# Low parts of the u table in the gate stage: every second block on GpSimd instead of VectorE

## What is computed

```python
a = jax.nn.gelu(jnp.einsum('td,tkd->tk', xt, u_tab[it]))   # it: 8 heads x 16 experts of 16384, per token
y = jnp.einsum('tk,tkd->td', gt * a, v_tab[it])
```

## Time and profile before

| what | value |
|---|---|
| median of 3 runs | 2208.14 us (2207.04 to 2209.24) |
| the profiled execution: its time, its span | 2208.77 us, 2207.0 us |
| busy over the span | PE 93%, DVE 69%, ACT 37%, POOL 31% |
| the chain that ended last | PE 72%, DMA 9%, DVE 8%, issue 5%, ACT 4%, POOL 1% |
| gate stage | from 943 to 1426 us of the span |

### The profile page before, as it was taken

The page is one execution under the profiler, slowest core; times in us unless marked ns, Lnnn a source line. Parts: engine busy times, 40 slices in busy tenths (PEclk is TensorE's granted clock), DMA queues, the critical chain, the costliest instruction groups (busy, mean ns, idle before and its releaser), DMA issues.

```text
span 2207.0 us, 28461 instructions
## 1 busy us (share of the span) xinstructions
PE 2043.3 (93%) x9877; PEld 1635.1 (74%) x9877; DVE 1524.7 (69%) x3164; ACT 822.6 (37%) x1507; POOL 693.4 (31%) x469
## 2 busy tenths in 40 slices
PE   6999999697998989988888889979999999999998
PEld 2554454544998989887787788878888888888886
DVE  4222315624689999988788877738877678778776
ACT  2111004223222323377777778723222232222222
POOL 0000001002223666543333322214434355545451
PEclk8999999798999999999999999989999999999999
DMA  9121204415111455579999988989999899999994
GB/s 336 61 77 38 82 0 152 153 72 200 39 39 53 157 180 159 157 274 350 344 358 358 347 308 316 333 334 340 398 338 346 289 348 328 347 334 343 335 344 164
DMA packets 183919, 526.01 MB, mean 238 GB/s; under 512 B 16775, under 2 KB 67111, under 8 KB 181256
## 3 DMA queue, kind: packets, MB, share of 16 engines
q1 hardware_dynamic: 128520, 323.41, 40.5%
q0 software_dynamic: 55296, 201.35, 25.5%
HBM read 460.48 MB, written 64.23 MB: 238 GB/s over the span
## 4 chain that ended last, share of the span: by engine, by line
PE 72%; DMA 9%; DVE 8%; issue 5%; ACT 4%; POOL 1%; SPq 0%; ACTq 0%; DVEq 0%; POOLq 0%
PE ps L1012 32%; PE ps L945 12%; DMA ugat<-in_u_rows,idxs 6%; PE ps L662 5%; DVE junk L1477 3%; PE ps L755 3%; PE ps L881 3%; PE ps L917 3%; PE ps L918 3%; PE ps L721 3%; PE ps L985 2%; DMA uraw<-in_u_t 2%; DVE eA L1495 2%; ACT uhi L1737 2%; DMA wring<-in_w_ada 2%
## 5 line engine op out<-in xcount | busy, mean ns | idle before, releaser
L945 PE MATMUL ps<-h2hi,uhi 128*128 128x384 f32 x1024 | 400.9, 392 | 39.3 <-issue 19.7
L1885 POOL DMA_INDIRECT ugat<-in_u_rows,idxs x256 | 272.6, 1065 | 520.4 <-DVE dots L1477 509.5
L1012 PE MATMUL ps<-vhi,whi 128*128 128x512 f32 x1024 | 399.2, 390 | 5.1 <-DVE wlo L1524 5.1
L1012 PE MATMUL ps<-vhi,wlo 128*128 128x512 f32 x1024 | 398.8, 389 | 0.0
L1012 PE MATMUL ps<-vlo,whi 128*128 128x512 f32 x1024 | 398.8, 389 | 0.0
L945 PE MATMUL ps<-h2lo,uhi 128*128 128x384 f32 x1024 | 351.9, 344 | 0.0
L945 PE MATMUL ps<-h2hi,ulo 128*128 128x384 f32 x1024 | 349.8, 342 | 0.0
L1815 ACT ACTIVATE vhi<-vraw 128x1024 fp32r<-128x1024 f32 x128 | 135.5, 1061 | 463.6 <-PE ps L1012 442.8
L1893 POOL DMA_INDIRECT vgat<-in_v_tab,idxs x128 | 217.1, 1696 | 220.5 <-DVE y L1535 177.6
L985 PE MATMUL ps<-eA,eB 128*128 128x128 f32 x1024 | 213.5, 291 | 55.0 <-DVE eA L1495 46.6
L985 PEld LDWEIGHTS ps<-eA,eB 128*128 128x128 f32 x1024 | 182.7, 194 | 93.9 <-DVE eA L1495 66.2
(11 more groups left out here) (275 smaller groups left out, 3063.2 us busy)
## 6 DMA issues: line engine op xcount, KB each, us to landing
uraw<-in_u_t SPq DMA_DIRECT2D x128, 512.0 KB
vraw<-in_v_tab SPq DMA_DIRECT2D x128, 512.0 KB
gate_scratch<-gst SPq DMA_DIRECT2D x16, 2048.0 KB
gin<-gate_scratch SPq DMA_DIRECT2D x32, 1024.0 KB
wring<-in_w_ada SPq DMA_DIRECT2D x12, 2048.0 KB, 10.3
gelu_scratch<-aout SPq DMA_DIRECT2D x128, 192.0 KB
ain<-gelu_scratch SPq DMA_DIRECT2D x32, 768.0 KB, 7.4
wring<-in_w_in SPq DMA_DIRECT2D x6, 2048.0 KB, 8.4
```

What stands on the lines that cost most here:

```text
L945: last = pe.matmul(ps[:, b % 4, 0:TA], w[:, b % 2, k, :], h[:, k, LP:LP + TA], start=(k == 0 and j == 0), stop=(k == KD - 1 and j == 2))
L1012: last = pe.matmul(ps[:, y_bank(t) + h, :], w[:, b, (t - 1) * P:t * P], v[:, b, h * 512:(h + 1) * 512], start=(start and j == 0), stop=(st ...
L1885: pool.indirect_dma_start(out=ugat[:, g % GSLOT], out_offset=None, in_=u_rows, in_offset=bass.IndirectOffsetOnAxis(ap=idxs[:, g // HK, g % ...
```

## The change

GpSimd makes the low part of every even block from 54 to 116 (32 of the 64 that VectorE made). Its program takes up the part of block n + 1 ahead of the gathers that follow the dots of block n. VectorE leaves these out, and ahead of each low part that it still makes it waits until GpSimd's last one is done; GpSimd waits likewise for VectorE's. One such wait stands before block 116's successor too. GpSimd's `split_u` is the function that it has for blocks 0 to 52; it waits for `uhi` of the block and for `h_full`.

```diff
+def pool_low(n):
+    return BLK_A < n <= BLK_C and n % 2 == 0
...
-                    if k == 3:
+                    if k == 3 and not pool_low(n + 1):
+                        dve.wait_ge(ulo_ready, n + 1)
                         split_u(n + 1, n + 1)
...
+            dve.wait_ge(ulo_ready, BLK_C + 1)
             for n in range(BLK_C, NBLK):
...
             pool.wait_ge(idx_ready, 2)
-            for g in range(GSLOT, NDOT):
+            for n in range(BLK_A, BLK_C):
+                if pool_low(n + 1):
+                    pool.wait_ge(ulo_ready, n + 1)
+                    split_u(n + 1, n + 1, False)
+                for g in dots_at(n):
+                    gather_u(g + GSLOT)
+            for g in range(dots_before(BLK_C) + GSLOT, NDOT):
                 gather_u(g)
```

## The result

The changed kernel takes 2243.55 us (median of 4, 2241.53 to 2246.82), the one before beside it 2207.59 us (2199.4 to 2209.24): a ratio of 1.0172 with an interval of 1.0149 to 1.0194. That is 36 us slower; forecast were 8.5 us, and at most 26. The profiled execution has a span of 2245.0 us, 38 us longer than before.

The account below looks back on a forecast made before the run. Bound: a 6.92 us loop over the low part in two-dot blocks, full VectorE in three-dot blocks, transfers near. +10.7 - 6.5 + 4.3 = +8.5 us on 2208.77 gave 2217.3 us; own range 2213 to 2225, 8-in-10 range 2200 to 2234.

Parts of the forecast that it names:

- What VectorE loses per subtraction: Gate stage: each GpSimd subtraction makes VectorE stand still for 2.07 us, tiles and dots alike.
- The gathers' constant 937 ns: Gather instructions took 936 to 937 ns in nearly all of 166 cases, though starting beside tiles; evidence against stopped tiles.
- Three-dot blocks: Gate blocks with three dots, 19 pairs: VectorE is full, odd blocks go from 6.92 to 7.6 us; +10.7 us.
- the cover by transfers: Three-dot pairs: a quarter cost nothing because transfers set the pace; +10.7 us with it, 14 without.
- Two-dot blocks: Gate blocks with two dots, 13 pairs: VectorE no longer idles for the high part, block about 6.4 us; -6.5 us.
- Lock and loop: Gate stage: subtractions stopping VectorE in three-dot pairs, +10.7 us, and the shortened wait chain in two-dot pairs, -6.5 us.
- the queue of GpSimd: Three-dot pairs: gathers queue behind the high-part wait and subtraction, short by 0.3 us; +4.3 us, at worst 28.
- of the six gathers in a pair only one is held back: Three-dot pairs: argument against the much slower rival; the one gather is issued some 2.9 us later.
- 7.1 us as the lead that a gather needs: Gather to its dot: shortest time the trace shows without a wait, against 6.5 us left after the change.
- Gathers late: Rival, GpSimd's gather queue: the queue effect at its worst on top of the rest, 2234 us; chance 0.14.

Follow-up runs that it names:

- both repairs: Changed kernel plus a fifth buffer for gathered rows and each odd block's first gather issued ahead of GpSimd's low part: 2206.87 us, ratio 0.9997.
- the queue alone: Kernel before, VectorE making every low part, GpSimd's gathers of odd gate blocks held until the next block's low part is there: 2229.12 us, ratio 1.0117.

## Why the prediction failed

- **The sign and the place were right, the size was not.** 36 us slower, forecast 8.5; outside the range of 2200 to 2234.
- **What VectorE loses per subtraction:** forecast 2.07 us, measured 2.05 over 32 of them. Tiles are stopped (28 times) as well as dots (4 times). The gathers' constant 937 ns, which was held against it, says nothing of tiles.
- **Three-dot blocks:** forecast 7.6 us for an odd one, measured 7.56. The even ones nearly stay (forecast 6.92, measured 6.98). Without the cover by transfers, which I took off, that is 22 x 0.64 = 14 us.
- **Two-dot blocks:** forecast 6.4 us, typical 6.61, some 5.97. The gain of typical blocks was 3 us, not 6.5: the last stretch has 10 such odd blocks, and I had counted 13 pairs. Of the 7 two-dot blocks of the first stretch only two (71 and 77) are odd, and they took 7.5 and 7.6 us. Lock and loop together: 13 us by the typical blocks, 8.4 by the medians with both repairs, forecast 4.2.
- **The failing step is the queue of GpSimd.** The forecast was "of the six gathers in a pair only one is held back", by 2.9 us, its dot 0.3 us short, nothing behind it touched: +4.3 us. Held alone, with exactly one gather due in each pair, the queue cost 23 us, and the changed kernel's loss over the lock's is as large or larger. So the count of held gathers alone does not explain it; the price of one was too low. Three things were wrong in that step. First, a line is not issued at once: a gather issued while a dot or VectorE's low part runs ends 0.81 to 0.83 us after it (34 of 34 cases in the changed kernel), so it takes 1.0 to 1.9 us, and the ones behind a held one go out 1.1 us late. Second, I left VectorE in the place in time that it had before. But in an odd block it no longer waits for the high part, so it runs ahead: when the subtraction is over, its second dot is over too. Two gathers are due then in 20 of 32 cases, one in 8; in the typical case they go out 4.3 and 3.7 us after their dots. Third, I took 7.1 us as the lead that a gather needs. The gathers of 956.75 and 958.07 were in time for the dots of 962.18 and 964.11, 5.4 and 6.0 us later, and that of 959.45 was not in time after 6.4 (965.86, when VectorE began to wait): what is short is not one fixed lead but the gathers in a bunch.
- **What came on top** was in no term: a late dot and a stopped tile in a row make TensorE stand still for 3 us, and soon after it runs at 1.2 GHz for three steps. Over the stage the clock is at that level for 27 us more than before. If TensorE set the pace in all of them, that would be 12 us (an estimate: 27 x (1 - 0.75 / 1.38)); how much of it is in the 21 us of stalls, no run shows.
- **The rivals.** "Gathers late" was the right mechanism; I gave it 0.14 and 2234, with one gather per pair. That transfers cover a quarter of the pairs was not borne out: the share of the DMA engines fell.
- How the loss divides is known by runs only roughly: the queue alone 23 us by the medians (19 to 33 by the ratio), both repairs leave 8 (2 to 12), the whole is 36 (33 to 43). The 5 us between the sum and the whole lie within these intervals. That late dots meeting stopped tiles make the loss larger than both apart is read from the timeline, not shown by a run. No run keeps the subtraction on GpSimd with tiles that it does not stop, so the lock's share is known only as what is left.

## What to carry to other kernels

An in-order queue that issues transfers is a resource of its own. When compute work with a wait is put in front of its transfers, count every transfer that becomes due while it waits, with the consumer where it will be after the change and not where it was. And ask first whether the step needs another engine or only another place in the order: here one number, and a buffer more for the transfers' lead, gave 25 us where the other engine cost 36.

## What was not expected of the hardware

- The issue of an indirect gather takes 0.94 us as a rule when it begins beside a tile, even if a dot starts meanwhile; in the gate stage of the changed kernel these take at most 1.02. When it begins beside a running dot or low part of VectorE, both with two inputs, it ends 0.81 to 0.83 us after that instruction: 34 of 34 times in the changed kernel, and both times that this happened in the kernel before (945.39 and 1238.28). In the kernel before, a gather follows 0.28 us behind its dot and so meets tiles; a gather that has lost this place meets dots. A subtraction of GpSimd, for its part, stops a tile of 0.34 us until it is over (2.57 us at most).
- One standstill of TensorE of 2.9 us cost another 1.6 us through the granted clock: three steps at 0.50 (972.41 to 976.06).
